# Feed-forwards by Strassen's scheme: seven block products in place of eight, tokens as the stationary operand

## The reference

```python
h = rmsnorm(x, g_ffn1_pre[i])                          # x: 256 x 1024
x = x + 0.5 * rmsnorm(swiglu(h, w1_gate[i], w1_up[i], w1_down[i]), g_ffn1_post[i])
def swiglu(x, w_gate, w_up, w_down):                   # 1024 x 2816 twice, 2816 x 1024
    return (jax.nn.silu(x @ w_gate) * (x @ w_up)) @ w_down
```

## Time and profile before

| | |
|---|---|
| median of 3 runs | 2944.19 us (2943.7 to 2945.88) |
| span of the profiled execution | 2949.8 us |
| PE busy | 2641.7 us, 90% of the span |
| DVE busy | 738.9 us, 25% |
| ACT busy | 478.6 us, 16% |
| GpSimd busy | 224.2 us, 8% |
| moved by DMA | 690.40 MB, 234 GB/s on average |

### The profile page before, as it was taken

How to read it: one execution, slowest core, us unless ns; L and a number is a source line. 1 busy time by engine, 2 the same in 40 slices (tenths; PEclk the granted TensorE clock), 3 DMA queues, 4 the chain that set the end, 5 groups by cost and what they waited for, 6 DMA issues and landing times.

```text
span 2949.8 us, 57534 instructions
## 1 busy us (share of the span) xinstructions
PE 2641.7 (90%) x24600; PEld 2000.0 (68%) x24600; DVE 738.9 (25%) x2009; ACT 478.6 (16%) x1135; POOL 224.2 (8%) x406
## 2 busy tenths in 40 slices
...
GB/s 273 182 191 123 136 245 168 186 161 201 199 183 114 163 179 220 190 156 147 164 60 29 32 242 411 400 418 419 420 414 207 74 87 179 401 420 419 420 419 307
DMA packets 271385, 690.40 MB, mean 234 GB/s; under 512 B 35983, under 2 KB 163774, under 8 KB 254782
## 3 DMA queue, kind: packets, MB, share of 16 engines
...
## 4 chain that ended last, share of the span: by engine, by line
PE 76%; DMA 12%; DVE 6%; issue 3%; ACT 2%; SPq 0%; ACTq 0%; POOL 0%; POOLq 0%; DVEq 0%
PE ps L682 19%; DMA arena<-in_moe_w_up 11%; PE ps L693 10%; PE ps L2421 5%; PE ps L1546 4%; PE ps L2924 3%; PE ps L1605 2%; PE ps L2396 2%; PE ps L2436 2%; PE ps L913 2%; PE ps L706 2%; PE ps L1073 2%; PE ps L2176 2%; PE ps L2885 1%; PE ps L2948 1%
## 5 line engine op out<-in xcount | busy, mean ns | idle before, releaser
L682 PE MATMUL ps<-arena 128*128 128x256 f32 x2560 | 568.6, 379 | 3.5 <-DVE arena L766 3.5
L682 PEld LDWEIGHTS ps<-arena 128*128 128x128 f32 x2560 | 482.8, 189 | 73.9 <-issue 4.1
L693 PE MATMUL ps<-arena 128*128 128x256 f32 x1408 | 318.4, 379 | 0.0
L693 PEld LDWEIGHTS ps<-arena 128*128 128x128 f32 x1408 | 264.9, 189 | 46.4 <-issue 8.4
L2421 PE MATMUL ps<-arena 128*32 128x128 f32 x6016 | 198.7, 292 | 61.2 <-issue 58.4
L2421 PEld LDWEIGHTS ps<-arena 128*32 128x32 f32 x6016 | 183.6, 118 | 71.1 <-issue 66.4
L2924 PE MATMUL ps<-arena 128*32 128x128 f32 x4096 | 139.5, 295 | 81.9 <-issue 80.0
L810 DVE TENSOR_TENSOR arena<-arena,ps 128x256 f32<-128x256 f32 x76 | 32.0, 421 | 638.8 <-ACT arena L776 634.0
L2924 PEld LDWEIGHTS ps<-arena 128*32 128x32 f32 x4096 | 125.9, 119 | 87.0 <-issue 85.6
L776 ACT ACTIVATE arena<-ps 128x256 f32<-128x256 f32 x76 | 29.1, 383 | 675.5 <-PE ps L682 675.5
L1546 PE MATMUL ps<-arena 128*128 128x256 f32 (+2 forms) x384 | 133.8, 526 | 0.0
...
## 6 DMA issues: line engine op xcount, KB each, us to landing
...
arena<-in_w_gate SPq DMA_DIRECT2D x44, 1024.0 KB, 5.3
arena<-in_w_up SPq DMA_DIRECT2D x44, 1024.0 KB, 7.8
arena<-in_w_down SPq DMA_DIRECT2D x44, 1024.0 KB, 5.0
arena<-in_w_in SPq DMA_DIRECT2D x12, 1024.0 KB, 5.4
```

What stands on the lines that cost most here:

```text
L682: last = pe.matmul(k.ps[:, T % 4, off:off + S], w[:, t, T % 2 * P:(T % 2 + 1) * P], h[:, t, :], start=(t == 0), stop=(t == KT - 1), skip_g ...
L693: last = pe.matmul(acc[:, t, :], d[:, T % 2, t * P:(t + 1) * P], k.hid[:, T % 4, :], start=(T == 0 and t % 2 == 0), stop=end, skip_group_c ...
```

## The change

Every product of the feed-forwards becomes a product of 2x2 blocks in the form of Strassen and Winograd, with seven block products P1 to P7 and sums of blocks ahead of them and behind. The tokens are cut in two halves n of 128, the inner dimension in two halves, the weights' columns in two halves m.

- **Gate and up.** The tokens are the stationary operand: per product 4 inner tiles (HK), 128 tokens, and a moving tile of 256 columns, 128 of gate beside 128 of up. A chunk is seven such products. Token sums T1 to T4 are made once for a feed-forward (`dve_token_sums`), weight sums S1, S2, S4 and one in place (number 3) for every chunk (`dve_chunk_sum`), one chunk ahead; those of chunk 0 are made in the stage before (`dve_first_sums`), or, in (0, 0), behind the token sums. P2 adds onto P1's bank, P3 onto P5's, P4 onto P7's; the other sums of products (57, u2, 22, 12, 21) are DVE's, from copies that ACT makes (`snap`).
- **Gated rows** come out token-major; silu and product use the row norm as a factor by row (`k.rcol`). PE turns the four 128x128 blocks of each chunk (`turn_hidden`) and ACT copies them to `k.hidT`; all 11 are kept.
- **Down** follows after all chunks: 11 pairs of hidden tiles, each with token sums (three instructions), four weight sums (`dve_pair_sums`) and seven products with 512 columns, into seven banks that stay open over all pairs.
- **The end.** DVE sums the seven banks to four blocks of the token-major result `k.Y`, ACT squares them, and a product with a diagonal matrix of the norm's factors (`pe_rows_back`) turns and scales at once; DVE multiplies by the gain and adds to `k.X1` in one instruction per tile. `pe_between` of the next stage moves ahead of it.
- **Row norm ahead**: ACT squares `k.X1` inside chunk 0, DVE adds behind the third sum of chunk 1's weights, PE sums behind P3 (`pe_token_norms`), and DVE's reciprocal stands ahead of the first gated product. GpSimd's `pool_prepare` falls away for feed-forwards.
- **Transfers**: three slots of 2 MB for gate and up, six of 1 MB for down, in the same memory; context rows, tables and modulation loads move by a few chunks.

```diff
+GU = ("P1", "P5", "P7", "P6", "P2", "P3", "P4")
+GU_BANK = {"P1": 0, "P2": 0, "P6": 1, "P5": 2, "P3": 2, "P7": 3, "P4": 3}
+TURNS = (0, 1, 4, 5, 2, 3)
+DN = ("P1", "P6", "P7", "P5", "P2", "P3", "P4")
+DN_BANK = {"P1": 2, "P6": 3, "P7": 4, "P5": 5, "P2": 6, "P3": 0, "P4": 1}
+PAIR_SLOTS = ((4, 5, 0, 1, 2, 3, 4, 5, 0, 1, 2), (2, 3, 4, 5, 0, 1, 2, 3, 4, 5, 3))
+LATE_PAIRS = ((0, 1, 2, 3, 4), (0, 1, 2, 3, 7))
+BACK_BANKS = (7, 4, 5, 6)
+MOD_BANK, HID_BANK = 6, 7
...
+def chunk_slot(f, c):
+    return (c + 2 * f) % 3
+def chunk_bank(c, i):
+    return TURNS[(4 * c + i) % 6]
...
+    for c in range(3):
+        for w in before[chunk_slot(f, c)]:
             sp.wait_ge(*w)
         gate_up(c)
...
+        sp.wait_ge(*s["gu"].at(l, f, c, "P4"))
+        if c + 3 < CHUNKS:
+            gate_up(c + 3)
+        else:
+            down(2 * (c - CHUNKS + 3))
+            down(2 * (c - CHUNKS + 3) + 1)
+    for i, p in enumerate(LATE_PAIRS[f]):
+        sp.wait_ge(*s["dn"].at(l, f, p, "P4"))
+        down(6 + i)
...
+    def product(c, j):
+        bank = chunk_bank(c, GU_BANK[j])
+        out = ps[:, bank, 0:256].rearrange("p (g f) -> p g f", g=2)
+        if j in ("P3", "P5", "P6"):
+            w = k.wsums[("P5", "P6", "P3").index(j)].rearrange("p (k g f) -> p k g f", k=HK, g=2)
+            weights = [w[:, t, :, :] for t in range(HK)]
+        else:
+            m, half = {"P1": (0, 0), "P2": (0, 1), "P4": (1, 1), "P7": (1, 0)}[j]
+            weights = [chunk_block(k, f, c, m, half)[:, :, t, :] for t in range(HK)]
+        for t in range(HK):
+            if c == 0 and j == "P1":
+                pe.wait_ge(*s["made"].at(l, name, t))
+            last = pe.matmul(out, tokens[j][:, t, :], weights[t], start=(t == 0 and j in ("P1", "P5", "P6", "P7")), stop=(t == HK - 1), skip_group_check=True)
+        last.then_inc(*gu.up(l, f, c, j))
+    def turn_hidden(c):
+        pe.wait_ge(*s["hid_done"].at(l, f, c, "21"))
+        if c > 0:
+            pe.wait_ge(*s["hid_out"].at(l, f, c - 1))
+        for m in range(2):
+            for n in range(2):
+                last = pe.transpose(ps[:, HID_BANK, (2 * m + n) * P:(2 * m + n + 1) * P], k.hidt[:, c % 2, n, m, :], k.c["ident"])
+        last.then_inc(*s["hid_turned"].up(l, f, c))
...
+        if c >= 2:
+            pe.wait_ge(*u.at(l, f, c - 2, "12"))
+        product(c, "P1")
+        pe.wait_ge(*s["w_sum"].at(l, f, c, 1))
+        if c == 0:
+            pe.wait_ge(*s["t_sum"].at(l, f, 1))
+        else:
+            pe.wait_ge(*s["hid_done"].at(l, f, c - 1, "11"))
+        product(c, "P5")
+        pe.wait_ge(*s["w_sum"].at(l, f, c, 3))
+        if c == 0:
+            pe.wait_ge(*s["t_sum"].at(l, f, 3))
+        else:
+            pe.wait_ge(*u.at(l, f, c - 1, "u2"))
+        product(c, "P7")
...
+        pe.wait_ge(*s["w_sum"].at(l, f, c, 2))
+        if c == 0:
+            pe.wait_ge(*s["t_sum"].at(l, f, 2))
+        if c >= 2:
+            pe.wait_ge(*u.at(l, f, c - 2, "21"))
+        product(c, "P6")
+        if c == 0:
+            pe_turn_between(k, l, name)
+        pe.wait_ge(*s["snap"].at(l, f, c, "P1"))
+        product(c, "P2")
...
+            pe_token_norms(k, l, f)
+            pe.wait_ge(*s["t_sum"].at(l, f, 4))
+        if mod is not None:
+            pe_modulation_out(k, l, mod, MOD_BANK, k.mrow, 0)
+        pe.wait_ge(*s["snap"].at(l, f, c, "P7"))
+        product(c, "P4")
...
+        for j in DN:
+            if p == 0 and j in free:
+                pe.wait_ge(*free[j])
+            if j == "P6":
+                pe.wait_ge(*s["t_sum"].at(l, f, "pair", p))
+            if j in summed:
+                pe.wait_ge(*s["w_sum"].at(l, f, "pair", p, summed[j]))
+                i = {"P5": 0, "P6": 1, "P3": 2}.get(j)
+                w = pair_block(k, f, p, 1, 0) if i is None else k.psums[p % 2][i]
+            else:
+                w = pair_block(k, f, p, *{"P1": (0, 0), "P2": (0, 1), "P4": (1, 1)}[j])
+            pe.matmul(ps[:, DN_BANK[j], :], rows[j], w, start=(p == 0), stop=(p == CHUNKS - 1), skip_group_check=True).then_inc(*dn.up(l, f, p, j))
...
+    pe.wait_ge(*s["y_sum"].at(l, f, "u2"))
+    pe_between(k, l, next_of(f))
+    pe_rows_back(k, l, f)
...
+    pe.wait_ge(*s["y_diag"].at(l, f, 1))
+    pe.wait_ge(*s["y_diag"].at(l, f, 0))
+    for g in range(4):
+        for i in range(2):
+            for n in range(2):
+                t = 2 * g + i
+                last = pe.matmul(k.ps[:, BACK_BANKS[g], (2 * i + n) * P:(2 * i + n + 1) * P], k.Y[:, n, t * P:(t + 1) * P], k.diag[:, n, :], start=True, stop=True, skip_group_check=True)
+        last.then_inc(*s["rows_back"].up(l, f, g))
...
+    def snap(c, j):
+        i = ("P1", "P5", "P7").index(j)
+        if c > 0:
+            act.wait_ge(*u.at(l, f, c - 1, "u2" if i == 0 else "57"))
+        act.wait_ge(*gu.at(l, f, c, j))
+        act.activation(k.snaps[i], ps[:, chunk_bank(c, GU_BANK[j]), 0:256], ACT.Copy).then_inc(*s["snap"].up(l, f, c, j))
+    def squared(i):
+        act.activation(k.sq[:, 2 * i:2 * i + 2, :], k.X1[:, 2 * i:2 * i + 2, :], ACT.Square).then_inc(*s["x_squared"].up(l, f, i))
+    def hidden_out(c):
+        act.wait_ge(*s["hid_turned"].at(l, f, c))
+        act.activation(k.hidT[c], k.banks(HID_BANK, 1, P), ACT.Copy).then_inc(*s["hid_out"].up(l, f, c))
...
+    S1, S2, S4 = (t.rearrange("p (k g f) -> p g k f", k=HK, g=2) for t in k.wsums)
+    out, a, b, op = {1: (S1, A[1, 0], A[1, 1], ALU.add), 2: (S2, S1, A[0, 0], ALU.subtract), 3: (A[1, 0], A[0, 0], A[1, 0], ALU.subtract), 4: (S4, A[0, 1], S2, ALU.subtract)}[i]
+    V.tensor_tensor(out, a, b, op).then_inc(*s["w_sum"].up(l, f, c, i))
...
+    every = hid.rearrange("p (a b) c -> p b a c", b=2)
+    V.tensor_tensor(ring[:, 0:2, :], every[:, 1, :, :], hid[:, 0:2, :], ALU.subtract).then_inc(*s["t_sum"].up())
+    V.wait_ge(*s["t_sum"].last())
+    V.tensor_tensor(ring[:, 2, :], hid[:, 3, :], ring[:, 0, :], ALU.subtract).then_inc(*s["t_sum"].up())
+    V.wait_ge(*s["t_sum"].last())
+    V.tensor_tensor(ring[:, 3, :], hid[:, 2, :], ring[:, 2, :], ALU.subtract).then_inc(*s["t_sum"].up(l, f, "pair", p))
...
+    for t in (0, 2):
+        V.wait_ge(*s["made"].at(l, name, t + 1))
+        V.tensor_tensor(T1[:, t:t + 2, :], hu[:, t:t + 2, P:S], hu[:, t:t + 2, 0:P], ALU.subtract).then_inc(*t_sum.up(l, f, 1))
+    V.wait_ge(*s["made"].at(l, name, KT - 1))
+    V.tensor_tensor(T3, hu[:, HK:KT, P:S], hu[:, 0:HK, P:S], ALU.subtract).then_inc(*t_sum.up(l, f, 3))
+    V.wait_ge(*t_sum.at(l, f, 1))
+    V.tensor_tensor(T2, hu[:, HK:KT, P:S], T1, ALU.subtract).then_inc(*t_sum.up(l, f, 2))
+    V.wait_ge(*t_sum.last())
+    V.tensor_tensor(T4, hu[:, HK:KT, 0:P], T2, ALU.subtract).then_inc(*t_sum.up(l, f, 4))
...
+        V.scalar_tensor_tensor(out, up, r, sil, ALU.mult, ALU.mult).then_inc(*done.up(l, f, c, which))
...
+        ahead = c + 1 if c + 1 < CHUNKS else None
+        if ahead:
+            V.wait_ge(*s[f"ff{chunk_slot(f, ahead)}"].at("ffn", l, f, ahead))
+            V.wait_ge(*gu.at(l, f, c, "P5"))
+            dve_chunk_sum(k, l, f, ahead, 1)
+            V.wait_ge(*s["w_sum"].last())
+            dve_chunk_sum(k, l, f, ahead, 3)
+        V.wait_ge(*s["snap"].at(l, f, c, "P7"))
+        V.tensor_tensor(k.p57, p5, p7, ALU.add).then_inc(*u.up(l, f, c, "57"))
+        V.wait_ge(*s["snap"].at(l, f, c, "P1"))
+        V.wait_ge(*gu.at(l, f, c, "P6"))
+        V.tensor_tensor(k.u2, p1, ps[:, chunk_bank(c, 1), 0:256], ALU.add).then_inc(*u.up(l, f, c, "u2"))
+        V.wait_ge(*u.last())
+        V.tensor_tensor(block(c, 1), k.u2, k.p57, ALU.add).then_inc(*u.up(l, f, c, "22"))
+        if ahead:
+            V.wait_ge(*s["w_sum"].at(l, f, ahead, 1))
+            dve_chunk_sum(k, l, f, ahead, 2)
+        else:
+            dve_pair_sums(k, l, f, 0)
...
+        V.wait_ge(*gu.at(l, f, c, "P3"))
+        V.tensor_tensor(block(c, 0), k.u2, ps[:, chunk_bank(c, 2), 0:256], ALU.add).then_inc(*u.up(l, f, c, "12"))
+        if ahead:
+            V.wait_ge(*s["w_sum"].at(l, f, ahead, 2))
+            dve_chunk_sum(k, l, f, ahead, 4)
...
+        V.wait_ge(*gu.at(l, f, c, "P4"))
+        V.tensor_tensor(k.c21, k.u2, ps[:, chunk_bank(c, 3), 0:256], ALU.add).then_inc(*u.up(l, f, c, "21"))
+        hidden(c, "t2")
+        hidden(c, "21")
...
+    dve_token_sums(k, l, f)
+    if (l, f) == (0, 0):
+        dve_first_sums(k, l, f)
+    for c in range(CHUNKS):
+        chunk(c)
...
+    V.tensor_tensor(u2, pc, bank("P6"), ALU.add).then_inc(*y.up(l, f, "u2"))
+    V.wait_ge(*y.last())
+    V.tensor_tensor(u3, u2, bank("P7"), ALU.add).then_inc(*y.up(l, f, "u3"))
+    V.tensor_tensor(u4, u2, bank("P5"), ALU.add).then_inc(*y.up(l, f, "u4"))
+    V.wait_ge(*y.at(l, f, "u3"))
+    V.tensor_tensor(k.Y[:, 1, 512:D], u3, bank("P5"), ALU.add).then_inc(*y.up(l, f, 1, 1))
+    V.tensor_tensor(k.Y[:, 0, 0:512], pc, bank("P2"), ALU.add).then_inc(*y.up(l, f, 0, 0))
+    V.wait_ge(*y.at(l, f, "u4"))
```

(22 more changed lines are left out.)

481 lines of the change are left out of this document (291 added, 190 removed).

## The result

The changed kernel takes **2862.44 us** (median of 4 runs, 2861.13 to 2864.14), the kernel before beside it 2943.94 (4 runs, 2939.94 to 2945.88). The ratio is 0.9726, 95% interval 0.9713 to 0.974: 81.5 us or 2.7% less. The forecast was 2879 with 2861 to 2899. Direction and mechanism came out, but 17 us more were gained than the sum had: the time lies 1.4 us above the range's lower end and outside the 2867 to 2893 that the forecast called its own. That it fell inside is the width of the range. The profiled execution has a span of 2860.1 us, 89.7 less than the one before; 5.6 of these lie behind the last feed-forward (1618.7 and 1613.1 us), where nothing was changed and where the other runs here scatter from 1609 to 1617.

A forecast was written before the change was run, and what follows sets the result against it. The prediction took PE's matmul time in the four feed-forwards to bound the kernel, with room on DVE and in transfers. Its terms summed to -64.9 us, from the median of 2944.19 to 2879 us, range 2861 to 2899.

The forecast's parts named there:

- products: PE in the four feed-forwards: block matmuls take 199.6 us instead of 228.6 each, 116.0 us less for four.
- transposes: PE in each feed-forward: 44 turns of gated rows at 0.119 us add 5.2 us, 20.8 for four.
- starts and clock: Feed-forward starts: 19.8 us lost to PE waiting for token tiles, T1 and the row norm, plus 8.0 for half clock.
- ends: Behind each last down product: next stage starts 8.0 us later in place of 6.8, 1.2 each, 4.8 us in all.
- first sums behind the mixer: Behind the mixer: first weight sums wait for their chunk and push the post-norm sum by 0.6 us, twice: 1.2.
- modulation waits: At L766, 10 modulation chunks each made PE wait 0.35 us for DVE; the new place has none: -3.5 us.
- DVE's cover: Steady chunks and pairs: DVE's 8.0 and 3.8 us hide behind PE's 12.6 and 6.0, costing zero; uncovered, 520 us.
- The hole itself: Feed-forward start: P1 is paced by token tiles, then P5 waits for T1 behind DVE's residual tiles; 3.9 us lost.
- The new hole looks like the second: Behind P1: a 3 us hole resembles an earlier thinly busy PE stretch followed by clock 0.50; 2 us per feed-forward.
- DVE setting the pace: Rival, chance 0.03, no change: at 14 us of DVE per chunk the 44 chunks lose 62 us, giving 2941.
- late handovers: Rival, chance 0.04, slower: 440 more product groups each handed over late, at 0.35 us +154, giving 3033 us.
- Nothing is lost at the edges: Rival, chance 0.09: no fall of the clock and a hidden norm, 8 + 4 us less, giving 2867.

## Why the prediction was right, and where its sum was off

| term | predicted | measured |
|---|---|---|
| products | -116.0 | -116.4 |
| transposes | +20.8 | +19.4 |
| starts and clock | +27.8 | +13.9 |
| ends | +4.8 | +1.7 |
| first sums behind the mixer | +1.2 | +3.3 |
| modulation waits | -3.5 | -2.5 |
| sum | -64.9 | -80.6 |

- **Products.** 308 x 0.433 + 77 x 0.859 = 199.5 us against 228.6, four times 29.1. That weights in two runs of 128 read as fast as one run was a guess without a row, and held.
- **Transposes.** 0.11 in place of 0.119: between products the end of a group doesn't add to it.
- **DVE's cover.** "Hidden by PE's own 12.6 and 6.0 us" is what the run with doubled sums shows directly. The margin in a chunk was read rightly; the run shows that the pairs' first step and the row norm have much less.
- **Starts: the step that failed.** It had three parts. The hole itself, "3.9 us lost": P5 starts 4.95 us behind P1, 1.73 of it work, so 3.2. The row norm, "0.6 more": it came without a wait in three of four. And the clock, "2 us for each": 1.7, and in the changed kernel's profile only once. From the first product to the first transposes the four take 22.8, 22.9, 24.5 and 22.9 us; without 40 products and the small pieces between them (18.2 in the first, 19.5 in the others) that is 4.6, 3.5, 5.1 and 3.5 lost, 16.6 in all. What I left out altogether is that the kernel before loses time at its first start as well: its 64 instructions take 16.53 us there and 14.07 elsewhere. The two stretches below, of 5.1 us each and of these products alone, hold 12 instructions and then 25: it starts at half pace. (The record of the granted clock begins only at 19.88, so the 1.00 of the first stretch says nothing.) That is 2.5 us, 2.7 with the other three starts, and makes 16.6 - 2.7 = 13.9.

```profile
14.80 16.53 PE L706 MATMUL ps<-arena 128*128 128x256 f32 x64
```

```profile
14.80:19.90 5.10, 5.10 (x12) 4.10 (x13) 1.00 1.07 351
19.90:25.00 5.10, 5.10 (x25) 4.44 (x24) 1.00 1.07 383
```

- **The clock as a chance, not a certainty.** "The new hole looks like the second" of the earlier trace rows holds half the time: 9 of 18. By these traces the term is an estimate of 1.7 x 3 x 0.5 = 2.6 for the three later starts, in place of 8.0, with both ends in the range.
- **Modulation.** A chunk with one is 2.95 us longer than one without, before 3.2: 10 x 0.25.
- **Ends.** +0.4 to 0.5 each, not 1.2: the diagonal is ready at 235.16, before PE ends the modulation products, and the first tile of the next stage is ready 3.7 us after the first turned-back product.
- **First sums.** "Push the post-norm sum by 0.6, twice": 2.2 and 1.0, since the post-norm's product now starts behind a wait of 2.08 and 0.86 where it followed the mixer's last product without one. The transfer lands 9.1 us after it is asked for and not in 7.8, and only 4 us ahead of the last mixer product. In layer 0 the edit that moves them gives back 2.3.
- **The rule weighed.** The Trainium skill (TensorE: Matmul & The Clock Gate, "The cost: per-tile semaphore tail") states 26.3 ns for each raise of packed tiles; by an estimate from it the raises of the change would cost 11 us and those of the run with a raise on each matmul 24. The second isn't there: the steady chunk is 12.56 us either way. The measurement decides, for f32 products that are not packed.
- **Rivals.** DVE setting the pace and late handovers need PE waits in steady chunks; there are none. One of the signs of being wrong did show: behind the mixer a weight transfer ends DVE's wait for the first sums (27.41 us), and with it PE's of 2.08. "Nothing is lost at the edges" took off only the clock and the row norm's part and came to 2867; the measured time lies below it, since the holes were shorter than 3.9, the ends cost 1.7 and not 4.8, and the old loss at the first start wasn't in any case.
- **Luck.** That the range held is in part luck: nearly all that was missed lay on one side (13.9 at the starts, 3.1 at the ends, 1.4 in the transposes), and "each feed-forward some 16 us shorter" was 20 to 23. Had the first sums and the modulation not missed the other way, by 3.1 together, the time would have been below 2861.

Measured items sum to -80.6. From the first product of the first feed-forward to the first product behind the last one the two profiled executions differ by 83.2, so 2.6 us stay without a place; the medians differ by 81.5.
